# Gate stage: the embedding's product from plain four-byte operands instead of three products of split operands

## The reference, cut to what matters

```python
gate = jax.nn.sigmoid(rms_norm(h, g_ple[i]) @ w_ple_gate[i])
h = h + gate * (p[i] @ w_ple_proj[i])
return rms_norm(h, g_final)
```

## Time and profile before

| | us |
|---|---|
| median of three executions | 3268.03 |
| lowest, highest | 3261.69, 3269.47 |
| the profiled execution, in whole | 3271.68 |
| its span in the trace | 3269.9 |

### The profile page before, as it was taken

How to read it: one execution, slowest core, us unless ns; L and a number is a source line. 1 busy time by engine, 2 the same in 40 slices (tenths; PEclk the granted TensorE clock), 3 DMA queues, 4 the chain that set the end, 5 groups by cost and what they waited for, 6 DMA issues and landing times.

```text
span 3269.9 us, 48938 instructions
## 1 busy us (share of the span) xinstructions
PE 3135.4 (96%) x17504; PEld 2697.0 (82%) x17504; DVE 1817.1 (56%) x3103; ACT 1557.0 (48%) x2824; POOL 1369.4 (42%) x1116
## 2 busy tenths in 40 slices
PE   8999999899999999997998999899989999999998
PEld 8988888788888889996887888687768888888787
DVE  5134343888888866665555765677534544552222
ACT  4011111777777768884235555555533333333332
POOL 2133331011111135772235666666666666665222
PEclk9999999999999999998999999899999999999999
DMA  5233335303030328854763766377586678665221
GB/s 170 93 108 119 126 119 164 70 21 85 21 85 20 89 71 199 181 149 120 244 214 132 248 223 191 128 238 258 184 256 199 201 234 268 202 198 205 66 79 55
DMA packets 467407, 493.43 MB, mean 151 GB/s; under 512 B 84064, under 2 KB 377312, under 8 KB 461920
## 3 DMA queue, kind: packets, MB, share of 16 engines
q1 hardware_dynamic: 463824, 484.02, 48.5%
q10 hardware_dynamic: 3344, 6.29, 0.8%
HBM read 322.05 MB, written 168.17 MB: 150 GB/s over the span
## 4 chain that ended last, share of the span: by engine, by line
PE 79%; DVE 6%; POOL 4%; DMA 4%; ACT 3%; issue 3%; SPq 1%; POOLq 0%; ACTq 0%; DVEq 0%
PE h_acc L136 6%; PE h_acc L137 6%; PE h_acc L138 6%; PE a_acc L138 5%; PE a_acc L136 5%; PE a_acc L137 5%; PE c_pv L844 5%; PE b_pv L984 4%; PE c_turned L833 3%; PE e_acc L136 3%; PE c_scores L825 3%; PE c_scores L826 3%; PE e_acc L137 3%; PE e_acc L138 3%; PE b_scores L1236 3%
## 5 line engine op out<-in xcount | busy, mean ns | idle before, releaser
L2297 POOL TENSOR_TENSOR h_u_lo<-h_u_raw,h_u_hi 128x512 fp32r<-128x512 f32 x224 | 377.0, 1708 | 206.3 <-ACT h_u_hi L2293 206.2
L136 PE MATMUL h_acc<-h_w_hi,h_u_hi 128*128 128x512 f32 x896 | 350.9, 392 | 12.5 <-ACT e_u L2043 6.3
L741 DVE TENSOR_REDUCE c_neg_half<-c_scores 128x1 f32<-128x1024 f32 x256 | 313.0, 1223 | 81.9 <-PE c_scores L826 81.9
L137 PE MATMUL h_acc<-h_w_lo,h_u_hi 128*128 128x512 f32 x896 | 350.3, 391 | 0.0
L138 PE MATMUL h_acc<-h_w_hi,h_u_lo 128*128 128x512 f32 x896 | 350.2, 391 | 0.0
L2391 DVE TENSOR_TENSOR h_h<-h_acc,h_h 128x512 f32<-128x512 f32 x224 | 154.2, 689 | 325.1 <-PE h_acc L138 320.5
L136 PE MATMUL e_acc<-e_b_hi,e_a_hi 128*128 128x512 f32 x768 | 304.6, 397 | 26.3 <-ACT e_u L2043 17.5
L698 ACT ACTIVATE c_e<-c_scores,c_neg_max 128x1024 f32<-128x1024 f32 x256 | 287.1, 1121 | 59.6 <-DVE c_neg_max L748 51.6
L137 PE MATMUL e_acc<-e_b_lo,e_a_hi 128*128 128x512 f32 x768 | 301.6, 393 | 0.0
L138 PE MATMUL e_acc<-e_b_hi,e_a_lo 128*128 128x512 f32 x768 | 301.3, 392 | 0.0
L844 PE MATMUL c_pv<-c_v,c_at 128*128 128x128 f32 x2048 | 270.1, 275 | 0.4 <-ACT c_o L712 0.4
(11 more groups left out here) (201 smaller groups left out, 7989.0 us busy)
## 6 DMA issues: line engine op xcount, KB each, us to landing
h_u_raw<-s_u SPq DMA_DIRECT2D x224, 256.0 KB, 3.5
s_u<-e_u SPq DMA_DIRECT2D x192, 256.0 KB, 3.1
s_qkt<-a_hl SPq DMA_DIRECT2D x128, 256.0 KB, 2.8
e_a<-w_up_dram SPq DMA_DIRECT2D x64, 512.0 KB, 4.8
h_w_raw<-s_t SPq DMA_DIRECT2D x32, 1024.0 KB, 7.9
h_w_raw<-w_down_dram SPq DMA_DIRECT2D x24, 1024.0 KB, 7.9
b_kt<-s_qkt SPq DMA_DIRECT2D x64, 256.0 KB, 9.5
e_t<-w_down_dram SPq DMA_DIRECT2D x32, 512.0 KB, 5.9
```

The lines of the kernel that those rows point to most:

```text
L136: nc.tensor.matmul(out, lhs_hi, rhs_hi, start=first, stop=False, skip_group_check=onto)
L137: nc.tensor.matmul(out, lhs_hi, rhs_lo, start=False, stop=False, skip_group_check=onto)
L741: nc.vector.tensor_reduce(neg_half[:, m, f:f + 1], bank(n, u), AX.X, ALU.max, negate=True).then_inc(S["halved"], 1)
L2297: self.nc.gpsimd.tensor_tensor(self.u_lo[q][s][:], self.u_raw[q][s][:], self.u_hi[q][s][:].bitcast(F32), ALU.subtract).then_inc(self.S["u_ ...
```

## The change

The embedding's operands are no longer split. `e_raw` (the weights as loaded) and `et` (the transposed block as ACT copies it out of `f_e_turned`, now a float32 tile) go into one matmul for a block c, where three stood. ACT's rounding of the weights, POOL's `e_lo`, DVE's `lo_e` and their semaphores go; ACT's per-tile cast becomes a copy of the same size. PE waits for ACT's copy (`et`) where it waited for DVE's rest (`e_lo`). The gate's own product is left as it was, and so are all transfers and the order of everything else.

```diff
-        self.e_lo = [place(kit, f"f_e_lo{c}", kb, [P, DM], F32R) for c, kb in enumerate((148.25, 188.5))]
-        self.e_hi = [place(kit, f"f_e_hi{c}", kb, [P, DM], F32R) for c, kb in enumerate((152.25, 192.5))]
...
-        self.et_hi = [place(kit, f"f_et_hi{k}", 80 + 2 * k, [P, PC, P], F32R) for k in range(2)]
-        self.et_lo = [place(kit, f"f_et_lo{k}", 81 + 2 * k, [P, PC, P], F32R) for k in range(2)]
+        self.et = [place(kit, f"f_et{k}", 80 + 2 * k, [P, PC, P]) for k in range(2)]
...
-    def lo_e(self, dve, t):
-        nc, S = self.nc, self.S
-        dve.wait_ge(S["e_hi"], t + 1)
-        view = lambda x: x[t % 2][:].rearrange("p c t -> p (c t)")
-        nc.vector.tensor_tensor(view(self.et_lo), self.e_turned[:, :D_PLE], view(self.et_hi).bitcast(F32),
-                                ALU.subtract).then_inc(S["e_lo"], 1)
...
         if t:
-            pe.wait_ge(S["e_lo"], t)
+            pe.wait_ge(S["et"], t)
...
-            def hi_e(t):
+            def copy_e(t):
                 act.wait_ge(S["e_turn"], t + 1)
                 if t >= 2:
                     act.wait_ge(S["emb_acc"], 2 * (t - 2) + 2)
-                nc.scalar.copy(self.et_hi[t % 2][:].rearrange("p c t -> p (c t)"),
-                               self.e_turned[:, :D_PLE]).then_inc(S["e_hi"], 1)
+                nc.scalar.copy(self.et[t % 2][:].rearrange("p c t -> p (c t)"),
+                               self.e_turned[:, :D_PLE]).then_inc(S["et"], 1)
...
             hi(0)
-            act.wait_ge(self.e_in, 32)
-            for c in range(PC):
-                nc.scalar.copy(self.e_hi[c][:], self.e_raw[c][:]).then_inc(S["e_whi"], 1)
             down.wait_product(act, LAST, 4, 1)
             square(0)
-            hi_e(0)
+            copy_e(0)
...
             self.means(dve, 0)
-            self.lo_e(dve, 0)
...
                     self.lo(dve, t + 1)
-                    self.lo_e(dve, t + 1)
                     self.means(dve, t + 1)
...
-            for c in range(PC):
-                pool.wait_ge(S["e_whi"], c + 1)
-                nc.gpsimd.tensor_tensor(self.e_lo[c][:], self.e_raw[c][:], self.e_hi[c][:].bitcast(F32),
-                                        ALU.subtract).then_inc(S["e_wlo"], 1)
             root(0)
...
                 if t == 0:
                     self.turn_e(pe, 0)
-                    pe.wait_ge(S["e_wlo"], PC)
-                pe.wait_ge(S["e_lo"], t + 1)
+                    pe.wait_ge(self.e_in, 32)
+                pe.wait_ge(S["et"], t + 1)
...
                     for c in range(PC):
-                        ins = matmul3(nc, self.emb_acc[:, g], self.et_hi[t % 2][:, c], self.et_lo[t % 2][:, c],
-                                      self.e_hi[c][:, cols], self.e_lo[c][:, cols], c == 0, c == PC - 1)
+                        ins = nc.tensor.matmul(self.emb_acc[:, g], self.et[t % 2][:, c], self.e_raw[c][:, cols],
+                                               start=c == 0, stop=c == PC - 1)
                     ins.then_inc(S["emb_acc"], 1)
```

More of the change, by code:

```diff
@@ L2497, in __init__ @@
         self.gain_in, self.e_in = kit.sem("f_gain_in"), kit.sem("f_e_in")
-        names = ("w_scaled w_hi w_lo e_whi e_wlo ssq mean rstd turn hi lo e_turn e_hi e_lo gate_acc emb_acc gate gated "
+        names = ("w_scaled w_hi w_lo ssq mean rstd turn hi lo e_turn et gate_acc emb_acc gate gated "
                  "h3 ssq2 mean2 rstd2 out")
@@ L2666, in _ @@
                     hi(t + 1)
-                    hi_e(t + 1)
+                    copy_e(t + 1)
                     square(t + 1)
```

## The result

The changed kernel takes 3279.63 us in the median of 8 executions (3276.02 to 3283.3); the kernel before took 3270.14 us beside it (8 executions, 3261.69 to 3273.16). The ratio is 1.003, 95% interval 1.0019 to 1.0041: slower by 9.5 us, between 6.2 and 13.4. That is inside the range and 0.5 us off the time named.

A forecast was written before the change was run, and what follows sets the result against it. PE's stream was taken to bound the gate stage: +11.5 us over sixteen tiles less 0.46 us in the first made +11.1 us, which on the median of 3268.03 us gave 3279.1 us, range 3271 to 3286.

The forecast's parts named there:

- What bounds: Gate stage, tiles 2 to 13: PE busy for 176.00 of 176.00 us, so only edits to PE's stream count.
- Two records a product: Embedding product on PE: each plain product is two passes, so eight records a tile replace twelve float32r matmuls.
- Two cycles a column: Plain embedding records take columns at half float32r speed: 0.431 us at 512 columns, eight 3.45 us for 2.73.
- Rival 1: Embedding's plain records take one cycle a column, 0.227 us each: faster, 3253 us; chance 0.09.
- Rival 2: Embedding's weight loads no longer hide under matmuls, 0.431 + 0.11 us a record: +25 us, 3293 us; chance 0.05.
- Rival 4: Embedding product makes one record instead of two, four of 0.431 us a tile: near 3251 us; chance 0.02.
- The first tile: Tile 0: PE waits for ACT's copy alone, not DVE's subtraction too, so its 0.97 us stop shortens: -0.46 us.
- Edits that bring nothing: Dropped ACT weight casts, POOL rests and DVE `lo_e` were hidden under PE's work or slack: worth nothing.
- The sum: Whole kernel: 11.5 us over sixteen tiles less 0.46 in the first, +11.1 us, giving 3279.1 us.
- The range: Whole kernel, 3271 to 3286 us: said to take the sum's bounds, half-clock stretches both ways and half the scatter.
- Rival 3, the clock: First two tiles: shorter stop and moved start spare half-clock stretches, -1.6 to -3.3 us, 3276 to 3277 us; chance 0.12.
- The chances: Whole kernel, against a 9.8 us threshold: slower 0.62, same 0.27, faster 0.11.

The follow-up runs named there:

- experiment 2: Changed kernel with all splits still made but not used by the product: gate stretch 264.12 us against the changed kernel's 264.11, median 3282.84 us.
- 4: Changed kernel with the embedding's plain product in pieces of 128 columns, 32 records a tile for 8 of 512: median 3282.89 us.
- 9: Changed kernel with the embedding's plain product in pieces of 64 columns, 64 records a tile: 3336.04 us in one execution.

## Why the prediction was right, point by point

- **What bounds.** PE's stream alone, in every tile. Right: PE is busy for all of a tile at 12.92, 13.82, 14.73, 15.44 and 18.87 us, and with the splits put back (2).
- **Two records a product.** Right: 128 records.
- **Two cycles a column.** This was the step that everything hung on, and the one with no row of its own width. Predicted 0.431 us, bounds 0.427 and 0.454; measured 0.429. Eight: 3.43 us for the 3.45 named. The reading that gave it, the order of loads and matmuls and not their distance, was confirmed by 64 and 128 columns (4 and 9). The 0.111 us that the value started from was the 0.11 us limit's, some 0.003 above the columns' own 0.108, which is why it came out 0.002 high. That true FP32 goes through the array four times, the Trainium skill's "FP8 and Floating Point Precision", section "TensorE Precision Notes", is borne out by time: two records at two cycles a column.
- **Rival 1** (0.227 us a record, 3253 us) fell with the first rows of the profile after, 0.429. The prediction noted that the Trainium skill's "TensorE: Matmul & The Clock Gate", section "Back-to-back issue gap", would have it come out as this rival has it, at about 0.216 us a record; for a plain record the measurement decides against that figure. The break-even distance beside it is 0.345 us, not 0.346, and nothing hangs on that. **Rival 2**, loads that no longer hide, too: the load's 0.11 us would have made 0.54. **Rival 4** fell with the count.
- **The first tile.** -0.46 us predicted; the stop went from 0.97 to 0.51, and ACT's copy took the 0.37 us of its cast.
- **Edits that bring nothing.** Right by experiment 2. DVE was put at 4.0 us a tile and was busy for 4.08.
- **The sum.** +11.1 against +10.96 in the gate stretch without half clock. A tile was put at 15.45 us and took 15.44. That the time named was hit to 0.5 us is luck in part: the kernel before was 2.1 us slower beside the changed one (3270.14) than in the median that the prediction built on (3268.03), and the difference of the medians was 1.6 us smaller than the sum.
- **The range,** 3271 to 3286, holds the result, but its top is not what it is said to be made of: the upper bound of the sum (3282.0) with 3.3 us of half clock and 3.9 of scatter would be 3289. 3286 is reached from the value itself, 3279.1.
- **Rival 3, the clock,** is where the prediction was loosest. Stretches at half clock do come and go, each worth about 1.6 us, but it tied them to the change's shorter stop and moved start. In the first pair they went against the change by 1.23 us, in the second they were absent from both; the stops did not differ between executions with and without them. As an effect of the change it was not shown; as scatter of the measurement it is real, beside some 3.6 us either way in when the stage starts.
- **The chances.** Slower beyond 9.8 us was given 0.62, and slower by less than that 0.27 (as "same"). The medians moved by 9.5 and, executed again, 8.7 us, so by this line it is the second that came, while the gate stretch moved by 11. The difference of one to two us is within the intervals, and nothing here shows it as a gain. The mechanism is shown all the same: it was given 0.84 in all.

## What to carry to other kernels

Where PE is the bound, count cycles per column and not instructions: one plain four-byte product replaced three float32r ones here and cost 0.86 us for 0.68 at 512 columns. The splits that it saves are worth something only if the engines that make them are on the path. A distance between short matmuls may have another limit than the columns (here 0.11 us a record, most likely the weight load); look at where loads stand between the matmuls, or at another width, before scaling it.

## What was not expected of the hardware

A plain record costs its two cycles a column and little more: 0.429 us for 0.427 at 512 columns. A float32r matmul costs more over its one cycle: 0.227 us for 0.213, 14 ns each, and that in the projection, the output product, the MLP and the gate alike. With 256 columns, in the projection, it takes 0.120 us for 0.107, so the surplus is the same at half the width. That is why the trade was 3.8 to 3 and not 4 to 3. Where the 14 ns come from was not looked into.
